# Gate rows in the latent attention, unnormalised differential weights and regrouped TensorE insertions in a hybrid decoder block

## What is computed

```python
shift, scale, gate = split(c @ w_ada + b_ada, 3)            # c is one vector; w_ada is 2048 x 6144
h = rms_norm(x, g_pre) * (1 + scale) + shift
p = h @ w_in                                                # 2048 x 11328, split into ten parts
# latent attention (MLA): 8 heads, 128 + 64 (rotary), keys and values from rms_norm(c_kv) @ w_ukv
y_mla = (softmax(qn kn' + qr kr') v * silu(gate_mla)) @ w_o_mla
# differential attention: 8 heads with two score maps each
a = softmax(s0) - lam * softmax(s1);  o = rms_norm(a @ v) * g_subln * (1 - lambda_init)
y_diff = (o * silu(gate_diff)) @ w_o_diff
y = (sigmoid(mg_mla) * y_mla + sigmoid(mg_diff) * y_diff) @ w_out
out = x + gate * rms_norm(y, g_post)
```

## Time and profile before

| what | value |
|---|---|
| median of 3 runs | 799.82 us (798.71 to 799.89) |
| the profiled execution | 798.76 us, of it 797.0 us span |
| ACT busy | 396.8 us (50%) |
| POOL busy | 129.5 us (16%), between 400 and 710 us of the span |
| moved by DMA | 190.23 MB, mean 239 GB/s |
| differential attention | about 425 to 573 us |

### The profile page before, as it was taken

One profiled execution on the slowest core, in us unless ns is written; L12 is line 12 of the kernel. 1 busy time (PEld: TensorE's weight loads), 2 busy tenths in 40 slices (PEclk: granted clock), 3 DMA queues, 4 the chain that ended last, 5 costly groups with the idle time before them and its releaser, 6 DMA issues.

```text
span 797.0 us, 9829 instructions
## 1 busy us (share of the span) xinstructions
PE 758.8 (95%) x3533; PEld 621.9 (78%) x3533; DVE 567.2 (71%) x805; ACT 396.8 (50%) x634; POOL 129.5 (16%) x149
## 2 busy tenths in 40 slices
PE   4689999999999999999999999989999999999995
PEld 3567888878888788888887777767888888888884
DVE  4789999899767755555545999888777667575454
ACT  4456646445566555444446465635344444444441
POOL 2000000000000000000005441454264252500000
PEclk9799999999999999999999999999999999999998
DMA  9999999999663575555456767677678778767642
GB/s 339 388 328 353 368 325 344 325 352 316 216 202 116 180 195 158 155 158 155 137 190 215 256 211 222 201 234 214 213 251 284 230 242 266 277 218 227 223 158 105
DMA packets 117947, 190.23 MB, mean 239 GB/s; under 512 B 9925, under 2 KB 42890, under 8 KB 117642
## 3 DMA queue, kind: packets, MB, share of 16 engines
q1 hardware_dynamic: 117776, 189.56, 72.5%
q10 hardware_dynamic: 122, 0.04, 0.0%
HBM read 187.47 MB, written 2.10 MB: 238 GB/s over the span
## 4 chain that ended last, share of the span: by engine, by line
PE 80%; DVE 11%; issue 3%; ACT 2%; DMA 2%; SPq 1%; POOL 1%; DVEq 0%; POOLq 0%; ACTq 0%
PE ps L1585 24%; PE ps L1589 24%; PE ps L1586 24%; DVE w_both L1333 3%; DVE ada_acc L1126 1%; SPq L416 1%; DMA ada_ring<-in_w_ada 1%; DMA w_raw<-in_w_in 1%; ACT w_both L885 1%; PE ps L1421 1%; PE ps L1430 1%; PE ps L1434 1%; PE ps L1377 1%; DVE yg L1355 1%; PE ps L1460 1%
## 5 line engine op out<-in xcount | busy, mean ns | idle before, releaser
L1333 DVE TENSOR_TENSOR w_both<-w_raw,w_both 128x1024 fp32r<-128x1024 f32 x248 | 304.4, 1235 | 140.9 <-ACT w_both L885 140.2
L885 ACT CAST w_both<-w_raw 128x1024 fp32r<-128x1024 f32 x248 | 259.3, 1051 | 278.4 <-PE ps L1589 219.8
L1585 PE MATMUL ps<-w_both,h_hi 128*128 128x512 f32 x704 | 284.2, 404 | 5.3 <-DVE w_both L1333 5.1
L1589 PE MATMUL ps<-w_both,h_lo 128*128 128x512 f32 x704 | 275.8, 392 | 0.6 <-DVE h_lo L1242 0.6
L1586 PE MATMUL ps<-w_both,h_hi 128*128 128x512 f32 x704 | 275.0, 391 | 0.0
L1585 PEld LDWEIGHTS ps<-w_both,h_hi 128*128 128x128 f32 x704 | 132.5, 188 | 37.4 <-issue 9.1
L1589 PEld LDWEIGHTS ps<-w_both,h_lo 128*128 128x128 f32 x704 | 132.5, 188 | 30.0 <-DVE h_lo L1242 1.1
L1586 PEld LDWEIGHTS ps<-w_both,h_hi 128*128 128x128 f32 x704 | 132.9, 189 | 26.5 <-issue 0.7
L1126 DVE SCALAR_TENSOR_TENSOR ada_acc<-ada_ring,cols,ada_acc 128x512 f32<-128x512 f32 x112 | 78.3, 747 | 1.7 <-DMA ada_ring<-in_w_ada 1.7
L535 POOL TENSOR_SCALAR gate_ring<-gate_ring,cols 128x512 f32<-128x512 f32 x28 | 50.6, 1808 | 58.1 <-DMA gate_ring<-in_w_ada 57.3
L1585 PE MATMUL ps<-w_both,o_hi 128*128 128x512 f32 x128 | 50.7, 396 | 0.0
(11 more groups left out here) (225 smaller groups left out, 721.3 us busy)
## 6 DMA issues: line engine op xcount, KB each, us to landing
w_raw<-in_w_in SPq DMA_DIRECT2D x177, 512.0 KB, 4.7
ada_ring<-in_w_ada SPq DMA_DIRECT2D x128, 256.0 KB, 6.3
gate_ring<-in_w_ada SPq DMA_DIRECT2D x32, 512.0 KB, 5.4
w_raw<-in_w_out SPq DMA_DIRECT2D x32, 512.0 KB, 4.0
w_raw<-in_w_o_mla SPq DMA_DIRECT2D x16, 512.0 KB, 4.3
w_raw<-in_w_o_diff SPq DMA_DIRECT2D x16, 512.0 KB, 5.7
w_raw<-in_w_ukv SPq DMA_DIRECT2D x8, 512.0 KB, 4.2
x_tok<-in_x SPq DMA_DIRECT2D x2, 1024.0 KB, 6.0
```

The lines of the kernel that those rows point to most:

```text
L885: act.copy(w_hi[:, p % RING, :], w_raw[:, p % RING, :]).then_inc(hi_done, 1)
L1333: dve.tensor_tensor(w_lo[:, p % RING, :], w_raw[:, p % RING, :], w_hi[:, p % RING, :].bitcast(F32), ALU.subtract).then_inc(lo_done, 1)
L1585: mm(o, lhsT=s_hi[:, k, q], rhs=hi, start=first and r == 0, stop=False)
L1589: ins = mm(o, lhsT=s_lo[:, k, q], rhs=hi, start=False, stop=last and r == tiles - 1)
```

## The change

1. **Gate rows.** All 64 row blocks of the gate part go to DVE alone (`gate_row`), from place 87 to 126, eight rows on five pieces: the first row of a place stands before the `w_both` of that piece, a second one behind it. SP's loads into `gate_ring` move there too (`gate_load_at`); the slots lie elsewhere in SBUF. POOL's part of it is gone. The four sums over partitions stay on PE; ACT copies 32 partitions of each (`act_gate_row`), and bias and gain are applied once for all four (`gate_finish`, place 141), from where 16 small DMAs spread the rows to all partitions.
2. **Differential weights.** `diff_weights` no longer normalises the two maps. It makes one ratio per row and adds the second map, scaled by it, to the first; the missing factor goes into the squares (`first_scale`) and, by one more instruction of POOL, into the inverse root.
3. **Places.** Latent heads: s, s + 4, s + 6, s + 8. Differential heads: s, s + 5, s + 7, s + 10. In each, three of the four places fall together with those of the neighbouring heads. `diff_weights` goes from place s + 8 to s + 7 on DVE; on the places where it meets `diff_out` of the head before it now stands ahead of it. The sigmoid of the latent merge gate is read two pieces later.
4. **Small ones.** `dve_ckv_lo` is four instructions instead of seven, and ACT's wait and copy behind it are gone (PE waits for the semaphore itself, in `group`). `o_lo` is one instruction instead of two or three. The weight lambda is kept negated, and a shift of the first map's exponent stands in for very large values.

The diff, cut to its core:

```diff
-        gate_ring = sb("gate_ring", [P, 2, PIECE], F32, r_a + 24 * KB)
+        gate_ring = sb("gate_ring", [P, 2, PIECE], F32, r_o_lo + 8 * KB)
...
-        mla_at = [(MLA0 + 4 * h, MLA0 + 4 * h + 3, MLA0 + 4 * h + 5, MLA0 + 4 * h + 7) for h in range(HEADS)]
-        diff_at = [(DIFF0 + 5 * h, DIFF0 + 5 * h + 6, DIFF0 + 5 * h + 8, DIFF0 + 5 * h + 11) for h in range(HEADS)]
+        mla_at = [(MLA0 + 4 * h, MLA0 + 4 * h + 4, MLA0 + 4 * h + 6, MLA0 + 4 * h + 8) for h in range(HEADS)]
+        diff_at = [(DIFF0 + 5 * h, DIFF0 + 5 * h + 5, DIFF0 + 5 * h + 7, DIFF0 + 5 * h + 10) for h in range(HEADS)]
...
-        GATE0, GATE_STEP = first_piece("mm", 0) + 5, 3
-        gate_parts_at = {GATE0 + GATE_STEP * k: (k,) for k in range(4 * (KT // 2))}
-        gate_end = [GATE0 + GATE_STEP * (8 * n + 7) for n in range(4)]
-        gate_sum_at = [gate_end[n] + (n > 0) for n in range(4)]
+        GATE0 = first_piece("ukv", 2) + 2
+        gate_row_at = [GATE0 + r * 5 // 8 for r in range(4 * KT)]
+        gate_load_at = {gate_row_at[2 * k] + 1: k for k in range(2 * KT)}
+        gate_sum_at = [gate_row_at[KT * n + KT - 1] + 1 for n in range(4)]
+        gate_rows_on = {}
+        for r, place in enumerate(gate_row_at):
+            gate_rows_on.setdefault(place, []).append(r)
+        POST0 = first_piece("mm", 0) + 14
...
+            def load_gate(k):
+
+                n, i = k // (KT // 2), k % (KT // 2)
                 if k >= 2:
-                    sp.wait_ge(gate_used, k - 1)
-                    sp.wait_ge(gate_used_pool, k - 1)
+                    sp.wait_ge(gate_used, 2 * (k - 1))
                 else:
-                    sp.wait_ge(pv_done, HEADS)
+                    sp.wait_ge(silu_ready, 4)
...
+            def spread_gate(n):
+
+                sp.wait_ge(gg_ready, 1)
+                rows = slice(n * P // 4, (n + 1) * P // 4)
+                for q in range(4):
+                    sp.dma_start(post_gain[q * P // 4:(q + 1) * P // 4, n * CH:(n + 1) * CH],
+                                 gate_rows[rows, :]).then_inc(post_in, 16)
...
+                if p in gate_load_at:
+                    load_gate(gate_load_at[p])
+                if p == POST0:
+                    load_bias_gain()
+                if POST0 + 10 <= p < POST0 + 14:
+                    spread_gate(p - POST0 - 10)
...
-                nc.gpsimd.tensor_tensor(rstd[:, k, :], variance[:, k, :], in_range[:, :], ALU.mult).then_inc(rstd_ready, 1)
+                nc.gpsimd.tensor_tensor(rstd[:, k, :], variance[:, k, :], in_range[:, :], ALU.mult).then_inc(head_root_ready, 1)
+                pool.wait_ge(head_root_ready, h + 1)
+                nc.gpsimd.tensor_tensor(rstd[:, k, :], rstd[:, k, :], first_scale[:, h % 2, 1, :], ALU.mult).then_inc(rstd_ready, 1)
...
-            eng.wait_ge(ckv_lo, 2)
-            act.copy(ckv_signal[:, 0:1], cols[:, 0:1]).then_inc(tr_copied, 2)
...
+        def act_gate_row(n):
+
+            def run(eng):
+                rows = slice(n * P // 4, (n + 1) * P // 4)
+                eng.wait_ge(gate_summed, n + 1)
+                act.copy(gate_rows[rows, :], ps[rows, 6, :]).then_inc(gate_copied, 1)
...
-            act_after[last_piece("mm", n) + 3].append(act_read(acc_of["mm", n], read_sigmoid(n)))
+            act_after[last_piece("mm", n) + 5].append(act_read(acc_of["mm", n], read_sigmoid(n)))
...
+                    ins = dve.scalar_tensor_tensor(out=ckvT_lo[:, k, :],
+                                                   in0=ps[:, 4 + (G_CKV + g) % 4, b * SEQ:(b + 1) * SEQ],
+                                                   scalar=cols[:, V_GKV + k:V_GKV + k + 1],
+                                                   in1=ckvT_hi[:, k, :].bitcast(F32), op0=ALU.mult, op1=ALU.subtract)
+                ins.then_inc(ckv_lo, 1)
...
+                if m < HEADS:
+                    ins = dve.tensor_tensor(o_lo[:, m, :], src, o_hi[:, m, :].bitcast(F32), ALU.subtract)
+                else:
+                    ins = dve.scalar_tensor_tensor(out=o_lo[:, m, :], in0=src, scalar=cols[:, NVEC:NVEC + 1],
+                                                   in1=o_hi[:, m, :].bitcast(F32), op0=ALU.mult, op1=ALU.subtract)
+                ins.then_inc(o_lo_ready, 1)
...
-                second = recip[:, m % 2, :].rearrange("p (b w) -> p b w", w=2)[:, :, 1]
-                link(eng, dve.tensor_scalar(second, second, lam[:, 0:1], None, ALU.mult))
-                spans = ((0, P), (P, KEYS))
-                for b, (lo, hi) in enumerate(spans):
-                    ins = dve.tensor_scalar(probs[:, m % 2, 1, lo:hi], probs[:, m % 2, 1, lo:hi],
-                                            recip[:, m % 2, 2 * b + 1:2 * b + 2], None, ALU.mult)
+                by_map = lambda x, w: x[:, m % 2, :].rearrange("p (b w) -> p b w", w=2)[:, :, w]
+                dve.tensor_scalar(first_scale[:, m % 2, 0, :], by_map(recip, 0), SQ_SCALE, None, ALU.mult)
+                dve.tensor_copy(first_scale[:, m % 2, 1, :], by_map(recip, 0))
+                link(eng, dve.scalar_tensor_tensor(out=ratio[:, m % 2, :], in0=by_map(recip, 1), scalar=neg_lam[:, 0:1],
+                                                   in1=by_map(sums, 0), op0=ALU.mult, op1=ALU.mult))
+                for b, (lo, hi) in enumerate(((0, P), (P, KEYS))):
+                    ins = dve.scalar_tensor_tensor(
+                        out=probs[:, m % 2, 0, lo:hi], in0=probs[:, m % 2, 1, lo:hi], scalar=ratio[:, m % 2, b:b + 1],
+                        in1=probs[:, m % 2, 0, lo:hi], op0=ALU.mult, op1=ALU.add)
+                ins.then_inc(weights_ready, 1)
...
+                for t in range(TOK):
+                    ins = dve.tensor_scalar(tmp[:, t * P:(t + 1) * P], ps[:, 7, t * P:(t + 1) * P],
+                                            first_scale[:, h % 2, 0, t:t + 1], SQ_CLAMP, ALU.mult, ALU.min)
...
+        def gate_row(r):
+
+            def run(eng):
+                n, k, t = r // KT, r // 2, r % 2
                 eng.wait_ge(gate_in[k % 2], 16 * (k // 2 + 1))
...
+                if r % KT == 0 and n >= 2:
+                    eng.wait_ge(gate_summed, n - 1)
+                add_rows(eng, ada_acc[:, n % 2, :], gate_ring[:, k % 2, t * CH:(t + 1) * CH],
+                         cols[:, V_C + r % KT:V_C + r % KT + 1], r % KT == 0, (gate_used, r), gate_used)
...
+        def gate_finish(eng):
+            eng.wait_ge(gate_copied, 4)
+            eng.wait_ge(bias_in, 16 * 8)
+            link(eng, dve.tensor_tensor(gate_rows[:, :], gate_rows[:, :], bias_gain[:, 0, :], ALU.add))
+            dve.tensor_tensor(gate_rows[:, :], gate_rows[:, :], bias_gain[:, 1, :], ALU.mult).then_inc(gg_ready, 1)
...
             s, t, v, g = diff_at[h]
+            dve_after[g + 4].append(dve_o_lo(HEADS + h))
+            dve_after[v + 4].append(head_squares(h))
+        for h in range(HEADS):
+            s, t, v, g = diff_at[h]
             dve_after[s + 4].append(diff_scores(h))
-            dve_after[s + 8].append(diff_weights(h))
-            dve_after[v + 4].append(head_squares(h))
-            dve_after[v + 5].append(diff_out(h))
-            dve_after[g + 4].append(dve_o_lo(HEADS + h))
+            dve_after[s + 7].append(diff_weights(h))
+        for h in range(HEADS):
+            dve_after[diff_at[h][2] + 5].append(diff_out(h))
...
+                rows = gate_rows_on.get(p, [])
+                for r in rows[:1]:
+                    gate_row(r)(eng)
...
+                for r in rows[1:]:
+                    gate_row(r)(eng)
...
+            for m, place in enumerate(mla_at + diff_at):
+                pe_after[place[3]].append(lambda m=m: transpose_out(m))
+                pe_after[place[2]].append(lambda m=m: values(m))
+            for m, place in enumerate(mla_at + diff_at):
+                pe_after[place[1]].append(lambda m=m: transpose_probs(m))
             for h in range(HEADS):
+                pe_after[mla_at[h][0]].append(lambda h=h: mla_scores(h))
+                pe_after[diff_at[h][0]].append(lambda h=h: diff_scores_pe(h))
```

183 lines of the change are left out of this document (63 added, 120 removed).

## The result

The changed kernel takes **788.66 us** (median of 4 runs, 788.19 to 788.86), the kernel before 799.86 us on the same chip (798.71 to 800.03): a ratio of 0.9866 [0.9855, 0.9878], 11.2 us less. Forecast was 791.2, range 788.3 to 797.0. The profiled executions stand at 788.86 us (span 787.1) and 798.76 us (span 797.0): 9.9 us between them. The one of before is among its lowest runs, the one of after is not, which is most of the difference between 11.2 and 9.9; what follows accounts for the 9.9.

A forecast was written before the change was run, and what follows sets the result against it. TensorE bounds the kernel (PE's matmuls busy 758.8 of 797.0 us), so only PE's waits and insertions can be won. Terms - 1.8 - 5.8 - 1.0 + 1.0 - 0.8 + 0.5 = - 7.9 us give 790.9 profiled, 791.2 as median; range 788.3 to 797.

The forecast's parts named there:

- the forecast as worked out: Whole kernel: the summed terms come out about as counted, 789 to 793 us; chance 0.62.
- Start of `ukv`: Start of `ukv`: PE's whole 1.84 us wait goes, minus 1.8 us, bounds 0 and 2.1.
- Differential attention: Differential attention: all listed PE waits go, minus 5.8 us (bounds 3 and 7.5), and minus 1.0 for waits too short to list.
- The gated output: Differential heads: new weights stand ahead of the gated output, so it comes late; plus 1.0 us, bounds 0 and 8 x 0.7.
- The slack of 0.7: Differential heads: 0.7 us left between the end of the gated output and PE coming for its transposes.
- Rival B: Differential heads: weights take 2.3 us, not 1.6, and PE waits for the gated output at all eight; 796 us, chance 0.12.
- Insertions: PE's stream: 16 fewer interruptions by small matmuls at about 0.05 us each; minus 0.8 us, bounds 0 and 1.6.
- Latent attention: Latent attention: DVE at 86% with the gate rows, some places late; plus 0.5 us, bounds 0 and 3.
- The circle: Latent attention: refilling and using both `gate_ring` slots takes 15.6 us against 17.5 for five pieces, so it closes by 1.9.
- The slack of 2.9 us: Latent attention: in head 6 the gated output ended 2.9 us before PE came for it; a row takes 0.75 of it.
- Rival A: Latent attention: two-slot `gate_ring` too slow as landings grow; at 6.4 us landing a 15 us loss, 806 us; chance 0.08.
- Rival C: Latent heads: DVE lags over 2.9 us behind a late gate load, 8 x 0.5 us of waits; 795 us, chance 0.13.

The follow-up runs named there:

- the idle load: 31 idle DVE rows and three idle POOL pairs per head added to the changed kernel's differential attention; 790.01 us, ratio 0.9893 to the kernel before.
- the clean run: Changed kernel with three insertions per latent head back, as before the change, and gate sums one place later; 789.33 us, ratio 0.9872 to the kernel before.

## Why the prediction was right

The median lies in the stated range, 0.4 us inside its better end, and just outside the band of 789 to 793 us that was called the forecast as worked out. The path was the one predicted; the sizes were all too careful.

**Start of `ukv`: 1.8 forecast, 2.0 to 2.1 measured**, alone and in the whole. Its four DVE instructions took 1.65 us where 2.0 stood in the sum, and PE was next in line, as written. The bound of 2.1, with the restart, was nearer than the term.

**Differential attention: 5.8 + 1.0 forecast, 7.6 measured.** All listed waits went. What was mis-sized is the 1.0 for waits too short for the list, with the slower matmuls behind each longer one: it is 1.8. Its cause was half right. The prediction let the load go and the waits with it, which the run with the rows' move alone confirms. It gave the new arrangement of the heads no part in that. By the traces this leaves PE more room for the weights (0.85 us and more, where the move alone has 0.05 at the tightest head), and under the idle load PE waits 0.3 us; whether it would have cured the waits of before by itself is open. The sum counted the gain once, so the number did not suffer. The two passes of the earlier trace rows, 2.08 us together, take 0.75 us now, and none is over 0.48.

**The gated output: plus 1.0 forecast, about 0.3 measured.** The slack of 0.7 was about right: at the eight heads it is 0.4, 0.8, 0.06, 1.1, 1.1, 0.4, 1.1 and 1.9 us. The third waits 0.3. The table loads that were to cost 0.3 to 0.6 us each did so once; weights of 1.35 us and not 1.6 paid for the others. Rival B was this with longer weights; the old weights brought it out with 0.5 us of wait at one head.

**Insertions: 0.8 forecast, about 0.9 in the account.** The trace of after has 60 insertions in place of 78, so 18 and not 16. For eight of them the clean run gives 0.4 to 0.6 us, so each is worth 0.05 to 0.08, where the earlier trace rows had 0.05.

**Latent attention: 0.5 forecast, 0.24 measured** in one profiled execution, none in the other. DVE's share was put at 86% and is 81%, since the estimate spread the rows evenly over 140 us and the stretch of the profile holds fewer of them. The circle was put at 15.6 us for five pieces with landings of 4.0 and 4.8; the landings are 3.8, 4.4 and 7.7 (least, middle, most; the two longest at 272 and 274 us, before the rows are due), and DVE waited for them 9.4 us in ten waits of up to 1.9. The slack of 2.9 us behind it is real: it is 2.2 to 3.1 at seven heads, and 0.05 or 1.0 at the first, where the distances stand in DVE's queue. The fit of the Trainium skill (DMA: Bandwidth & Descriptors, Anatomy of one DMA) comes to 3.2 us for 512 KB by estimate; the section gives it for DMAs that GpSimd issues, and these are SP's. It is below every landing of these runs, of which the least is 3.6.

**Rival A** was rightly a rival: one row of delay for each load gives 20 us. **Rival C** happens, rarely: the late load in one profiled run cost 2.6 us in one place, not 0.5 at each of eight. That the single runs of the changed kernel spread over 787.8 to 789.4 us may come from this; its two traces differ at the first latent head by only 0.24 us, so it is not shown.

The sum was 790.9 for the profiled execution and 788.86 came: 2.0 us too careful, from 0.8 (short waits and restarts), 0.7 (gated output), 0.1 (insertions), 0.3 (latent attention) and 0.2 (`ukv`), all in the same direction, since each unknown was put on its costly side.

## What to carry to other kernels

Before work is moved off a stretch where an engine waits, work out both what it weighs there and how much slack its new place has per piece; a load of 81% on DVE cost nothing at seven heads because the tile that PE asks for stood 2 to 3 us ahead of it, and at the first, which had less, nothing, 0.24 us or, with a late load, 2.6 us. One more row of delay per load cost 20 us. Undoing all but one part of a change shows that part to be enough, not that the others are idle: put the load back into the changed kernel as well, and look whether it meets the same instructions as it did. When an experiment comes out at its rival's number, read its list of waits before believing it; two of these runs measured a misplaced gate sum and one a late load.
